# Gated DeltaNet heads: the next head's projections placed between the steps of the present one, two products a level instead of three, gated output kept in DRAM

## The reference, cut to what matters

```python
q, k, v = silu(short_conv(h @ w_in)) per head          # 8 heads, dk 128, dv 256
q, k = l2norm(q) * dk**-0.5, l2norm(k)
m = where(strict, (k*beta) @ k.T * decay, 0)            # per chunk and direction
tmat = inverse(m + I)                                   # lower triangular
v_new = tmat @ (beta*v) - tmat @ (beta*k*exp(gc)) @ s   # scan over chunks
o = (q*exp(gc)) @ s + (q @ k.T * decay) @ v_new
s = s * exp(gc_last) + (k*exp(gc_last - gc)).T @ v_new
out = (rmsnorm(o_fwd + o_bwd) * silu(z)) @ w_out        # z: 2 more tiles of h @ w_in
```

## Time and profile before

| | us |
|---|---|
| median of 3 runs (6446.47 to 6452.47) | 6452.19 |
| the profiled execution | 6448.12 |
| its span | 6446.3 |
| PE, DVE, ACT, POOL busy | 4846.8, 4659.9, 1666.9, 1619.9 |

### The profile page before, as it was taken

One profiled execution on the slowest core, in us unless ns is written; L12 is line 12 of the kernel. 1 busy time (PEld: TensorE's weight loads), 2 busy tenths in 40 slices (PEclk: granted clock), 3 DMA queues, 4 the chain that ended last, 5 costly groups with the idle time before them and its releaser, 6 DMA issues. The chain is left out here.

```text
span 6446.3 us, 86274 instructions
## 1 busy us (share of the span) xinstructions
PE 4846.8 (75%) x28546; PEld 4396.5 (68%) x28546; DVE 4659.9 (72%) x8489; ACT 1666.9 (26%) x2238; POOL 1619.9 (25%) x1060
## 2 busy tenths in 40 slices
PE   7677776754369999888577777777744379998887
PEld 1366676754369898888566666667744379998886
DVE  0255555369879999999455555555379879999998
ACT  0022222211343333332221111221211433333332
POOL 0000000011036666665000000000011046666664
PEclk9788888877689999999798888898977699999998
DMA  7211100100179999998000000000110289999996
GB/s 270 89 33 37 37 27 17 53 30 29 69 283 369 366 369 349 349 349 311 29 24 24 24 21 16 20 21 20 52 37 22 104 333 369 369 369 343 347 352 243
DMA packets 397661, 1059.23 MB, mean 164 GB/s; under 512 B 36464, under 2 KB 143216, under 8 KB 390384
## 3 DMA queue, kind: packets, MB, share of 16 engines
q0 software_dynamic: 147456, 536.94, 22.5%
q1 hardware_dynamic: 249968, 519.27, 22.2%
HBM read 998.92 MB, written 57.15 MB: 164 GB/s over the span
## 5 line engine op out<-in xcount | busy, mean ns | idle before, releaser
L1996 POOL DMA_INDIRECT dense_rows<-in_peer_u_rows,dense_expert_ids x512 | 760.8, 1486 | 891.2 <-DVEq L2012 473.4
L1604 POOL TENSOR_TENSOR top_w_lo<-top_w,top_w_hi 128x1024 fp32r<-128x1024 f32 x32 | 95.3, 2997 | 3423.2 <-ACTq L1572 3423.2
L1996 POOL DMA_INDIRECT dense_rows<-in_peer_v,dense_expert_ids x512 | 763.5, 1491 | 457.9 <-DVE sparse_acc L2052 349.8
L1906 PE MATMUL psum<-dense_a_hi,dense_v_hi 128*128 128x384 f32 x2048 | 704.6, 344 | 146.3 <-DVE residual L2039 143.7
L1891 PE MATMUL psum<-peer_in_hi,dense_u_hi 128*128 128x384 f32 x2048 | 697.8, 341 | 97.3 <-PE psum L1906 48.8
L1906 PE MATMUL psum<-dense_a_hi,dense_v_lo 128*128 128x384 f32 x2048 | 690.4, 337 | 0.0
L1906 PE MATMUL psum<-dense_a_lo,dense_v_hi 128*128 128x384 f32 x2048 | 690.1, 337 | 0.0
L1891 PE MATMUL psum<-peer_in_hi,dense_u_lo 128*128 128x384 f32 x2048 | 688.3, 336 | 0.0
L1891 PE MATMUL psum<-peer_in_lo,dense_u_hi 128*128 128x384 f32 x2048 | 688.0, 336 | 0.0
L2052 DVE SCALAR_TENSOR_TENSOR sparse_acc<-dense_rows,dense_weights,sparse_acc 128x1024 f32<-128x1024 f32 x512 | 656.2, 1282 | 37.1 <-DVE sparse_acc L2052 8.9
L2047 DVE CUSTOM_DVE_ANT_0 dense_rows<-dense_rows,sparse_in 128x1024 f32<-128x1024 f32 x512 | 605.1, 1219 | 0.0
(11 more groups left out here) (336 smaller groups left out, 10277.1 us busy)
## 6 DMA issues: line engine op xcount, KB each, us to landing
dense_u<-in_peer_u SPq DMA_DIRECT2D x256, 512.0 KB, 5.9
dense_v<-in_peer_v SPq DMA_DIRECT2D x512, 256.0 KB, 7.9
mod_w<-in_w_mod SPq DMA_DIRECT2D x24, 2048.0 KB, 7.7
gate_matrix<-gate_stage SPq DMA_DIRECT2D x12, 4096.0 KB, 11.2
dense_g<-gate_matrix SPq DMA_DIRECT2D x128, 384.0 KB, 7.9
gdn_w<-in_gdn_w_in SPq DMA_DIRECT2D x48, 512.0 KB, 3.3
ssd_w<-in_ssd_w_in SPq DMA_DIRECT2D x40, 512.0 KB, 3.3
top_w<-in_peer_w_q SPq DMA_DIRECT2D x32, 512.0 KB, 3.6
```

What stands on the lines that cost most here:

```text
L1604: nc.gpsimd.tensor_tensor(wlo[:, s].rearrange("p k n -> p (k n)"), w[:, s].rearrange("p k n -> p (k n)"), whi[:, s].rearrange("p k n -> p ...
L1906: last = nc.tensor.matmul(ps[:, 2 + t, 0:ND], w[:, q % 4, cut], x[:, at], start=(e == 0 and m == 0), stop=(e == XB - 1 and m == 2))
L1996: pool.indirect_dma_start(out=rows[:, f % NBUF], out_offset=None, in_=table, in_offset=bass.IndirectOffsetOnAxis(ap=eid[:, c, p:p + 1], ax ...
```

## The change

**Order.** The body of head i now also computes the projections of head i+1. One unit is one 128-row piece (six matmuls); `fill(count)` puts units between the steps on PE's queue. The two z tiles belong to head i itself, then come q, k, v of the next head. Before the loop the first head's q, k, v are projected, and the last head stands behind the loop with the z tiles alone. Slots 0 and 1 of PSUM carry projections and sums, slots 2 and 3 the head's steps.

**Levels.** `xi` is no longer updated by a product: PE transposes `xt` at each level (one record for each chunk), and ACT copies the needed half of its columns. The mask is applied after the product, to the half of the columns that a level changes, and the update touches that half.

**Smaller parts.** ACT makes the high parts of the weights and POOL the low ones; ACT scales `kg` and `rhs` for the scan, with two buffers. Lengths are computed as one value a token: sums by PE with the squares as stationary operand, roots and reciprocals of 128x10 and 128x5, spread over the partitions by a product with the identity. POOL sets `xi` and `xt` to the identity. `y` goes to DRAM head by head, and the output projection loads it as eight pieces ahead of its weights. The mask table is half as wide.

PE:

```diff
+                def fill(count):
+                    for _, u in zip(range(count), units):
+                        unit(i, u, kind)
...
+                pe.wait_ge(k_unit, i + 1)
+                pe.wait_ge(q_unit, i + 1)
+                pe.wait_ge(o_taken, GVT * (i + 1))
+                for slot, moving, made in ((2, kf[:], kk_made), (3, q, qk_made)):
+                        last = nc.tensor.matmul(ps[:, slot, cs(c)], kf[:, cs(c)], moving[:, cs(c)],
                                                 start=True, stop=True)
+                    last.then_inc(made, 1)
+                fill(2)
                 pe.wait_ge(stat_ready, i + 1)
+                for dr, taken in ((FWD, kk_taken), (BWD, qk_taken)):
+                    pe.wait_ge(taken, i + 1)
+                    for c in range(NC):
+                        last = nc.tensor.matmul(ps[:, 2 + dr, cs(c)], st[:, GG, c, dr:dr + 1].to_broadcast([P, P]),
+                                                k.c(NEGS[dr][2]), start=True, stop=True)
+                    last.then_inc(g_made[dr], 1)
+                fill(6)
+                pe.wait_ge(convolved, GCONV * (i + 1))
...
+                    s = 2 + c % 2
+                    for t, src in enumerate((kf[:], qkv[:, 2], qkv[:, 3])):
+                        last = nc.tensor.transpose(ps[:, s, t * P:(t + 1) * P], src[:, cs(c)], k.c("ident"))
+                    last.then_inc(turn_made, 1)
+                    if c == 3:
+                        fill(2)
+                fill(2)
+                pe.wait_ge(turned, NC * (i + 1))
                 for dr in range(2):
+                    pe.wait_ge(ba_ready[dr], i + 1)
                     for c in range(NC):
+                        last = nc.tensor.matmul(ps[:, 2 + dr, cs(c)], ba[:, dr, cs(c)], k.c("ident"),
+                                                start=True, stop=True)
+                    last.then_inc(lx_made[dr], 1)
+                fill(2)
+                for n in range(1, LEVELS):
                     for dr in range(2):
+                        pe.wait_ge(x_ready[dr], LEVELS * i + n)
+                        for c in range(NC):
+                            last = nc.tensor.transpose(ps[:, 2 + dr, cs(c)], xt[:, dr, cs(c)], k.c("ident"))
+                        last.then_inc(tr_made[dr], 1)
+                    fill(1)
                     for dr in range(2):
+                        pe.wait_ge(xi_ready[dr], NX * i + n)
                         for c in range(NC):
+                            last = nc.tensor.matmul(ps[:, 2 + dr, cs(c)], ba[:, dr, cs(c)], xt[:, dr, cs(c)],
+                                                    start=True, stop=True)
+                        last.then_inc(lx_made[dr], 1)
+                    for dr in range(2):
+                        pe.wait_ge(lx_ready[dr], NX * i + n)
+                        for c in range(NC):
+                            last = nc.tensor.matmul(ps[:, 2 + dr, cs(c)], xi[:, dr, cs(c)], lx[:, dr, cs(c)],
+                                                    start=True, stop=True)
+                        last.then_inc(xt_made[dr], 1)
                 pe.wait_ge(init_loaded, 32 * (i + 1))
                 for m in range(NS):
                     pair = steps[2 * m:2 * m + 2]
                     for dr, c in pair:
                         if c != CTXC:
                             if m:
                                 pe.wait_ge(state_ready[dr], (NS - 1) * i + m)
+                            else:
+                                pe.wait_ge(x_ready[dr], LEVELS * (i + 1))
+                            nc.tensor.matmul(ps[:, 2 + dr, 0:GDV], kf[:, cs(c)], state[:, dr, c],
+                                             start=True, stop=True).then_inc(ks_made[dr], 1)
+                    fill(1)
                     for dr, c in pair:
                         pe.wait_ge(rhs_ready[dr], NS * i + m + 1)
+                        nc.tensor.matmul(ps[:, 2 + dr, 512:512 + GDV], xt[:, dr, cs(c)], rhs[:, dr, m % 2],
+                                         start=True, stop=True).then_inc(vn_made[dr], 1)
+                    fill(2)
                     for dr, c in pair:
+                        pe.wait_ge(vn_ready[dr], NS * i + m + 1)
                         if c != last_of[dr]:
+                            nc.tensor.matmul(ps[:, 2 + dr, 0:GDV], kg[:, dr, m % 2], vn[:, dr, c],
+                                             start=True, stop=True).then_inc(kv_made[dr], 1)
+                    fill(1)
...
+                    last.then_inc(o_made, 1)
+                fill(GTILES * KT)
+                if more:
+                    qksum(i, kind)
+                pe.wait_ge(osq_ready, GVT * (i + 1))
```

DVE:

```diff
+                each = [ap.rearrange("p (c b two s) -> p c b two s", c=NC, two=2, s=1 << n)[:, :, :, 1 - dr]
+                        for ap in (lx[:, dr], ps[:, 2 + dr, 0:T])]
+                mask = bcast(masks[:, dr, n].rearrange("p (b s) -> p b s", s=1 << n), 1, each[0].shape)
+                done = nc.vector.tensor_tensor(each[0], each[1], mask, ALU.mult)
...
+            def update(i, n, dr):
+                x = pairs(xt[:, dr], n, 1 - dr)
+                if n:
+                    dve.wait_ge(xt_made[dr], NX * i + n)
+                    step = pairs(ps[:, 2 + dr, 0:T], n, 1 - dr)
+                else:
+                    step = pairs(lx[:, dr], n, 1 - dr)
+                nc.vector.tensor_tensor(x, x, step, ALU.subtract).then_inc(x_ready[dr], 1)
...
+                        level(i, n, dr)
+                    if n == 1:
+                        dve.wait_ge(aqk_exp, i + 1)
+                        dve.wait_ge(qk_taken, i + 1)
+                        nc.vector.tensor_tensor(aqk[:], aqk[:], bcast(qk, 1, [P, 2, T]), ALU.mult)
+                    if n == 2:
+                        nc.vector.tensor_tensor(qg[:], qg[:], bcast(q, 1, [P, 2, T]), ALU.mult)
...
+                scan(i, 0)
+                scan(i, 1)
+                if more:
+                    taps(i, 2)
+                scan(i, 2)
+                scan(i, 3)
+                if more:
+                    taps(i, 3)
+                scan(i, 4)
+                if more:
+                    taps(i, 4)
+                    taps(i, 5)
+                    lengths(i)
+                dve.wait_ge(ro_rooted, i + 1)
+                nc.vector.reciprocal(ro[:], ro[:])
...
+                if more:
+                    k_length(i)
+                dve.wait_ge(z_ready, GVT * (i + 1))
+                dve.wait_ge(obc_made, i + 1)
...
+                    last = nc.vector.tensor_tensor(zs[:, v], zs[:, v], ps[:, 1, 0:T], ALU.mult)
+                last.then_inc(slots.free[1], 1)
...
+                    q_length(i)
+                for v in range(GVT):
+                    nc.vector.scalar_tensor_tensor(zs[:, v], ps[:, 2 + v, 0:T], gain[:, v:v + 1], zs[:, v],
+                                                   ALU.mult, ALU.mult).then_inc(o_taken, 1)
+                dve.drain()
+                dve.sem_inc(y_ready, 1)
```

ACT and POOL:

```diff
+                nc.scalar.copy(kk, ps[:, 2, 0:T]).then_inc(kk_taken, 1)
...
+                for c in range(NC):
+                    act.wait_ge(turn_made, NC * i + c + 1)
+                    nc.scalar.copy(tok[:, c], ps[:, 2 + c % 2, 0:(1 + GVT) * P]).then_inc(turned, 1)
+                gate(i, 0)
+                if more:
+                    cast(i, 2)
+                act.wait_ge(eye_ready, i + 1)
+                for n in range(NX):
+                    for dr in range(2):
+                        act.wait_ge(tr_made[dr], NX * i + n + 1)
+                        nc.scalar.copy(pairs(xi[:, dr], n, dr), pairs(ps[:, 2 + dr, 0:T], n, dr)
+                                       ).then_inc(xi_ready[dr], 1)
+                    if n == 2:
+                        gate(i, 1)
+                        if more:
+                            cast(i, 3)
+                    if n == 3:
+                        prescale(i, 0)
+                    if n == 4:
+                        prescale(i, 1)
+                if more:
+                    act.wait_ge(conv_ready, i + 2)
+                    middle(i, 2)
+                    cast(i, 4)
+                prescale(i, 2)
+                if more:
+                    act.wait_ge(aqk_ready, i + 1)
+                    silu(i, 2)
...
+                for v in range(GVT):
+                    act.wait_ge(o_made, GVT * i + v + 1)
+                    nc.scalar.activation(osq[:, v], ps[:, 2 + v, 0:T], ACT.Square, scale=float(GDV) ** -0.5
+                                         ).then_inc(osq_ready, 1)
+                if more:
+                    silu(i, 4)
+                    middle(i, 5)
+                    cast(i, 7)
+                    silu(i, 5)
+                    roots(i)
+                act.wait_ge(osum_made, i + 1)
+                nc.scalar.activation(ro[:], ps[:, 1, 0:T].rearrange("p (c o) -> p c o", o=P)[:, :, 0], ACT.Sqrt,
```

(72 more changed lines are left out.)

631 lines of the change are left out of this document (305 added, 326 removed).

## The result

The changed kernel took 6119.19 us (median of four runs, 6116.5 to 6126.17) against 6450.95 for the kernel before beside it: ratio 0.9488, 95% interval 0.9472 to 0.9505. It is 5.1% faster; the forecast was 6150 with a range of 6085 to 6230. The same kernel timed again later took 6121.96 (five runs, 6116.44 to 6130.71). The profiled execution took 6126.17 us.

A forecast was written before the change was run, and what follows sets the result against it. A head was taken as bound by its chain of hand-overs, with PE having most work. 6448.1 - 1380 + 50 + 2 + 99 + 17 + 7h with h = 130 gave 6146 us, scaled to 6150; 8-in-10 range 6085 to 6230.

The forecast's parts named there:

- T = 5236 + 7h: Whole profiled execution in us: everything outside the seven looped heads is 5236, plus seven times h; 6146 forecast.
- h: Time of one looped head, forecast as 130 us: lead-in, levels, scan, output and turn-over, and clock.
- 50 + 2: Start of the heads' stage: 50 us for the first head's weights, projections and lengths, 2 us for window edges.
- Lead-in 22: From a head's start to the first level's product, masked and subtracted: products, decay sums, differences, exponentials, transposes; 22 us.
- clock 3.5: One granted-clock fall a head in the turn-over: 2 us lost at the next head's start, 1.5 in small products.
- The rival: POOL and DVE in each other's way: POOL's subtractions each hold up a DVE operation; h 133 to 147, chance 0.05.
- Levels 43: The levels after the lead-in: six of 6.9 us, set by PE, plus 1.5 for two DVE products; 43 us.
- Scan 33: The five scan steps with four units each, set by PE, plus convolutions and a first-product wait; 33 us.
- output 15: Behind the scan: 72 output records (8.0 us) and the last eight units (7.0 us).
- turn-over 13.5: Head's end: a chain of taps, SiLU, root, reciprocal, spreading, scalings, gate, outputs and hand-overs with little under it; 13.5 us.
- It comes from what PE has beside its waits: Source of the gain: not less PE work (113 us a head, as before) but work placed beside PE's waits.
- reciprocals of 8.15 us and 4.15 become 0.2 each: Turn-over: DVE's two wide reciprocals shrink to 0.2 us each, named as where the change saves.

The follow-up runs named there:

- e3: Changed kernel with the ten transposes of a level made as ten products with the identity; 6170.64 us, ratio 0.9565.
- e4: Changed kernel with DVE's update of a level (not the first) over all 640 columns, which makes the inverse wrong; 6140.49 us, ratio 0.9519.
- e1: Changed kernel with the 48 projection units of a head gathered in two blocks instead of strewn between steps; 6174.85 us, ratio 0.9568.
- e5: Kernel before the change, with each wide reciprocal replaced by filling the same columns with a constant; 6415.95 us against 6450.01 beside it, ratio 0.9945.
- e9: Changed kernel plus twelve unused products on PE in the turn-over, where PE waits for the outputs; 6122.76 us.
- e10: Changed kernel with the first two units of a head's z tile ahead of its key products instead of behind them; 6116.88 us.
- e12: Changed kernel with rebuilt turn-over, ACT's third weight cast moved, two early z units, and the output projection's first weight block loaded ahead of its sources; 6084.76 us.
- e14: e12 plus two z units moved from the first two levels into the lead-in; 6067.71 us, ratio 0.9409.

## Why the prediction was right, and where it wasn't

**The sum.** T = 5236 + 7h gives 6116 with the measured h of 125.7, and the profiled execution took 6126. h was forecast as 130, inside its own range of 124 to 136. The first loop pass began 57.0 us behind the window's edge (50 + 2 forecast; the stage itself began 5.8 us later, in unchanged code), the last head took 96 (99), the output projection started 16 us later (17 forecast, and 0.7 more than counted by the window's edges). The phases behind it, unchanged as well, took 7.4 us more in this execution. 5.0 - 2.9 + 0.7 + 7.4 is the distance from 6116 to 6126. That the total came within 20 us of 6146 is in part luck: the heads were 30 us shorter than forecast, and 13 us came from code that the change does not touch.

**Lead-in 22 plus clock 3.5.** Measured 25.3 on average (24.7 in the head of the first fence). The clock's share was mis-sized (2.1 on average), and 1.6 us of POOL against DVE were in no term. The rival had this mechanism right, one meeting a head of six possible, at 1.6 us where it had 3.

**Levels 43.** Measured 40.7. This is the largest miss: 6.69 a level for 6.9, and the two 128x1280 products added 0.5 us together, not 1.5, since most of their 1.5 us each lies beneath PE's two products. That the stage is PE's was right (e3), with the end of the second update on the path (e4), as forecast. The half-width operations took 0.49 us, where I used 0.55.

**Scan 33, output 15, turn-over 13.5.** Measured 31.0, 15.4, 13.2 (the windows of the first fence). POOL's identity copies took 2.5 us for both, not up to 9, its subtraction 2.4.

**What the steps meant.** The prediction got the size by adding up the new kernel's stretches, so it could be right without knowing which part of the change earned it. Two of its sentences on that don't hold as they stand. "It comes from what PE has beside its waits" is true of less than half: strewing brings 7.9 of 47 us a head (e1), and the wait ahead of the levels, which e1 fills too, 9.75. And "reciprocals of 8.15 us and 4.15 become 0.2 each" stands there as a saving of the turn-over, though only the second was ever on the path: e5 gives 4.3 of 12.3 us. The rest lies in the levels (8.30 to 5.81 without units), the scan steps (5.2 to 3.84), the stall at each head's start (14 us a head, now 3.3) and the granted clock (about 8 us a head, the estimate under the first fence). These overlap and don't add up to 47 by themselves. How they divide among narrower operations, the new duties of ACT and POOL and the order of the turn-over was not tried part by part.

**What stays open.** Whether the 1.79 us in e9 is PE's return, and why DVE stands only 0.64 us at its return to the loop's start instead of 3.19: no run separates it.

## What to carry to other kernels

Before crediting an overlap, find a stretch of the same kernel that runs without it (here the last head) and compare its period: if the strewn work costs its full price there, the stage is bound by the engine it is strewn on. That speaks for that stage alone: elsewhere in the head the z units filled a wait of 9.75 us. A long operation on a busy-looking engine is worth only the time in which the next engine stands still for it; read that wait first. And removing one gap can hand its wait and its clock fall to the next, so look at the next gap as well (e10's units alone brought 0.4 us a head; two more units in the gap behind them brought 2.3, e12 to e14). Whether those two would do it without the first two was not tried.

## What the runs showed of the hardware

- A 32-bit product of 32 moving columns takes as long as one of 128 with 128x128 stationary data: 276 and 275 ns, and a series of 20 took 2.31 and 2.50 us. Narrowing bought 0.2 us of 2.5 (two records a product).
- A DVE operation of 0.49 us with two SBUF inputs took 2.05 beside a POOL subtraction of 2.40; with one input in PSUM it kept 0.49.
- A fall of the granted clock to 0.50 (1.2 GHz) that lasts 6.8 us costs 2.6 us here, and in the changed kernel it differs from head to head (none at 3328, 3.4 us long at 3452, 6.8 us in the next four, read in windows of 0.2 us) though their instructions are the same.
